# Attention by pairs of heads, and the out projection's first weights loaded during attention

## The chip, the cores and the metric

The kernel runs on one NeuronCore of a Trainium2 chip. The metric is the device time of one execution in microseconds (us); lower is better. The engines named below are TensorE (PE, matmuls; PEld is its weight load), VectorE (DVE), ScalarE (ACT), GpSimd (POOL) and SyncE (SP, which issues the DMAs). All run in parallel, each works through its own list in order, and they wait for each other on semaphores.

## The reference

Two layers of a decoder step in float32, for a prompt of 1024 tokens and 8 sample sequences of 4 new tokens each, all with the same weights. What matters here is the attention half of the mixer. Each token has 4 heads with a query of 128 values without rotation (nope) and 64 rotated values (rope); the keys come from a shared latent of 256 values and one rotated key of 64 that all heads share.

```python
s = einsum('bqhd,bkd->bhqk', q, lat) * scale          # causal, scale = (128 + 64) ** -0.5
p = softmax(s, axis=-1)
o = einsum('bhqk,bkr->bqhr', p, vals)                 # then W_uv, giving 128 values per head
x = x + concat([hm, ha], axis=-1) @ lw['w_out']       # hm: 4 mLSTM heads, ha: 4 attention heads
```

The sample tokens attend to 1024 past rows each, read from a paged cache through a page table (8 pages of 128 rows per sequence), and to the new rows of their sequence.

## The kernel before

The kernel keeps all activations with features on the 128 partitions and tokens along the columns (1024 prompt columns and 32 sample columns, NT = 1056). `build_program` (L2264) runs a loop over the two layers; each layer is a list of phases (`mix_projection`, `mla_prepare`, `mla_attend`, `out_projection`, `conv_ffn`, `layer_embedding`), and between phases all engines meet at a barrier (L142, L150), so that nothing of a phase starts before the one ahead is done. The residual x lies in DRAM during the mixer.

`mla_attend` (L1404) does the attention of the prompt in 32 blocks: 4 heads, and for each 8 query tiles i of 128 queries, which see (i + 1) * 128 keys. The list `blocks` (L1436) has all tiles of a head, then the next head. The order of the work is written out by hand per engine. For block n:

- PE, `scores(n)` (L1472): for each piece of up to 512 keys a nope matmul (L1480, contraction over 128 rows) and a rope matmul (L1481, over 64 rows, on partitions 0 to 63 for even heads and 64 to 127 for odd ones) into a PSUM bank. Blocks alternate between two sets of two banks. `scores(n + 1)` is issued ahead of the rest of block n.
- DVE, `maxima(n)` (L1684): the causal mask on the diagonal tile (L1689), the row maximum (L1694) and its scaling (L1696).
- ACT (L1671): the exponential with the row sum. DVE (L1734, L1736): the reciprocal of the sum and the product with it.
- PE, `turned(n)` (L1495): each 128x128 tile of the probabilities is transposed (L1502), up to four into a bank; ACT, `transposed(n)` (L1621), copies each group of up to four out (L1627).
- PE, `values(n)` (L1485): one matmul per tile (L1491) into bank 6; DVE, `output(n)` (L1699), copies the result into `cat` (L1702).

An fp32 matmul is two records in the trace (two LDWEIGHTS and two MATMUL); a transpose is one.

Between these blocks `sample(n)` puts the sample tokens' attention into the same lists, in steps that all use PSUM bank 7. Two groups of four sequences take 11 steps each (GAP), the first at block FIRST = 8. Step 0 does the new scores, steps 1 and 2 the past scores (L1540, L1543, which need the cached pages), step 3 the softmax, steps 4 to 6 transposes (L1554), 7 and 8 the past values (L1567), 9 and 10 the heads' outputs (L1577, L1586). `absorbed` (L1506), at block 1, prepares the sample queries.

SP loads the pages with `load_pages` (L1394): for each sequence eight page numbers are read (L1397), then eight DMAs issued (L1402). The first four sequences come at the start; the keys of the other four after the first group's past scores (`past_done` 2), their latents after the first group's past values (`so_done` 1), into the same four page tiles.

`out_projection` (L1748) multiplies the 8 head outputs in `cat` with w_out. Products are made of two halves in a reduced format, three matmuls each (`product3`, L208): the high half of weights and activations is a copy by ACT, the low half a subtraction by DVE. `WeightRing` (L170) stages four weight jobs of 1 MB (JW = 2048 columns) in two slots. SP loads jobs 0 and 1, then x (4.2 MB), then the rest (L1763 to L1767); ACT splits job 0 (L198), then the 8 heads (L1773), DVE subtracts (L204, L1787), and PE's first job (L210) starts with the first head's low half. Job 1's subtraction on DVE stands behind the arrival of x (L1789).

## Time and profile before

| what | us |
|---|---|
| median of 3 runs | 3328.66 |
| lowest and highest of them | 3320.07, 3329.58 |
| the profiled execution | 3329.29 |
| its span in the trace | 3327.5 |
| PE busy (share of the span) | 3087.8 (93%) |
| DVE, ACT, POOL busy | 1524.3, 1067.3, 144.3 |
| mean granted TensorE clock, share of full | 0.958 |
| attention, layer 1 and layer 2 | 183.6, 186.6 |

The trace has one execution of the program. Times count from the start of the span. The first layer's attention lies at 416.9 to 600.5, the second's at 2052.3 to 2238.9. PEclk is the clock that TensorE was granted: 1.00 is 2.4 GHz, 0.50 is 1.2 GHz. Matmuls overlap in the engine, so the distance from one start to the next is the cost of one in a dense stretch, not its duration. An idle time is that of the engine just before the instruction, with what ended it behind the arrow.

### The profile page before, as it was taken

How to read it: one execution, taken by the hardware profiler on the slowest of the kernel's cores; microseconds unless marked ns; L12 is line 12 of the kernel's file. 1: busy time of each engine (PE TensorE's matmuls, PEld its weight loads, DVE VectorE, ACT ScalarE, POOL GpSimd, SP SyncE). 2: the span in 40 equal slices, each digit the busy share in tenths (PEclk: the TensorE clock that was granted, in tenths of full speed). 3: DMA queues.
4: the chain of work that ended last, by engine and by line, in shares of the span. 5: the costliest groups of instructions: out<-in, count | busy, mean ns of one | idle time of the engine just before them, and what ended most of it. 6: DMA issues, size and time to landing. Idle time of an engine off the chain costs nothing. (4 is left out here: it accounts for less than half of the span.)

```text
span 3327.5 us, 49163 instructions
## 1 busy us (share of the span) xinstructions
PE 3087.8 (93%) x19219; PEld 2874.2 (86%) x19219; DVE 1524.3 (46%) x2458; ACT 1067.3 (32%) x1982; POOL 144.3 (4%) x260
## 2 busy tenths in 40 slices
PE   4999999889999999988989999989899999999887
PEld 4998755789999999988989986559899999999886
DVE  4223643345454554447351345434554544454653
ACT  4323332324333323334242342322432323233341
POOL 0000300000000000000000012000000000000000
PEclk9999999889999999998989988989899999999988
DMA  5101252211111111102131023421111111111023
GB/s 212 52 26 44 86 172 70 103 56 51 39 39 52 46 44 51 39 18 90 40 123 41 16 99 101 133 60 81 68 40 50 51 39 51 39 39 51 6 103 131
DMA packets 60916, 220.53 MB, mean 66 GB/s; under 512 B 6922, under 2 KB 26890, under 8 KB 45842
## 3 DMA queue, kind: packets, MB, share of 16 engines
q1 hardware_dynamic: 60690, 217.27, 18.5%
q8 instruction: 172, 2.82, 0.4%
q14 instruction: 54, 0.44, 0.0%
HBM read 189.72 MB, written 27.52 MB: 65 GB/s over the span
## 5 line engine op out<-in xcount | busy, mean ns | idle before, releaser
L210 PE MATMUL psum<-h_high,conv_ffn_weight_parts 128*128 128x352 f32 x2112 | 690.4, 327 | 21.9 <-DVE h_low L315 14.3
L212 PE MATMUL psum<-h_high,conv_ffn_weight_parts 128*128 128x352 f32 x2112 | 686.7, 325 | 0.0
L211 PE MATMUL psum<-h_low,conv_ffn_weight_parts 128*128 128x352 f32 x2112 | 682.6, 323 | 0.0
L1990 DVE SCALAR_TENSOR_TENSOR conv_sum<-u_padded,vectors,conv_sum 128x1024 f32<-128x1024 f32 x176 | 226.1, 1285 | 595.1 <-ACT conv_sum L1939 582.6
L210 PEld LDWEIGHTS psum<-h_high,conv_ffn_weight_parts 128*128 128x128 f32 x2112 | 400.8, 190 | 24.9 <-issue 22.0
L211 PEld LDWEIGHTS psum<-h_low,conv_ffn_weight_parts 128*128 128x128 f32 x2112 | 399.3, 189 | 0.0
L212 PEld LDWEIGHTS psum<-h_high,conv_ffn_weight_parts 128*128 128x128 f32 x2112 | 397.1, 188 | 0.0
L210 PE MATMUL psum<-g_parts,conv_ffn_weight_parts 128*128 128x352 f32 x1056 | 345.3, 327 | 27.1 <-DVE g_parts L2001 16.3
L212 PE MATMUL psum<-g_parts,conv_ffn_weight_parts 128*128 128x352 f32 x1056 | 343.1, 325 | 0.0
L211 PE MATMUL psum<-g_parts,conv_ffn_weight_parts 128*128 128x352 f32 x1056 | 342.8, 325 | 0.0
L2009 DVE TENSOR_TENSOR x<-x,psum 128x352 f32<-128x352 f32 x528 | 255.5, 517 | 118.3 <-PE psum L212 117.9
L1935 ACT ACTIVATE u_padded<-psum 128x352 f32<-128x352 f32 (+1 forms) x264 | 120.2, 455 | 541.0 <-PE psum L212 541.0
L210 PEld LDWEIGHTS psum<-g_parts,conv_ffn_weight_parts 128*128 128x128 f32 x1056 | 199.9, 189 | 33.5 <-issue 16.8
L210 PE MATMUL psum<-h_high,_projection_weight_parts 128*128 128x352 f32 x576 | 192.5, 334 | 14.3 <-DVE h_low L315 14.3
L1948 ACT ACTIVATE g_parts<-conv_sum 128x1056 fp32r<-128x1056 f32 x44 | 47.8, 1087 | 486.9 <-PE psum L212 404.6
L211 PEld LDWEIGHTS psum<-g_parts,conv_ffn_weight_parts 128*128 128x128 f32 x1056 | 199.8, 189 | 0.0
L212 PEld LDWEIGHTS psum<-g_parts,conv_ffn_weight_parts 128*128 128x128 f32 x1056 | 198.9, 188 | 0.0
L212 PE MATMUL psum<-h_high,_projection_weight_parts 128*128 128x352 f32 x576 | 188.1, 326 | 0.0
L211 PE MATMUL psum<-h_low,_projection_weight_parts 128*128 128x352 f32 x576 | 187.7, 326 | 0.0
L1939 ACT ACTIVATE conv_sum<-psum,vectors 128x352 f32<-128x352 f32 x264 | 170.5, 646 | 0.1
L204 DVE TENSOR_TENSOR conv_ffn_weight_parts<-conv_ffn_weight_stage,conv_ffn_weight_parts 128x2048 fp32r<-128x2048 f32 x66 | 151.1, 2290 | 23.9 <-ACT conv_ffn_weight_parts L198 23.9
L210 PE MATMUL psum<-heads_high,_projection_weight_parts 128*128 128x352 f32 x384 | 126.0, 328 | 24.5 <-DVE heads_low L1787 24.5
(330 smaller groups left out, 5389.5 us busy)
## 6 DMA issues: line engine op xcount, KB each, us to landing
conv_ffn_weight_stage<-w_up_dram SPq DMA_DIRECT2D x44, 1024.0 KB, 4.8
conv_ffn_weight_stage<-w_down_dram SPq DMA_DIRECT2D x22, 1024.0 KB, 4.8
_projection_weight_stage<-w_in_dram SPq DMA_DIRECT2D x18, 1024.0 KB, 4.8
pages<-cache_dram SPq DMA_DIRECT2D x64, 288.0 KB, 4.2
pages<-cache_dram SPq DMA_DIRECT2D x64, 160.0 KB, 2.5
mix_work<-x_residual SPq DMA_DIRECT2D x16, 528.0 KB, 3.8
x<-x_residual SPq DMA_DIRECT2D x2, 4224.0 KB, 17.0
x_residual<-x SPq DMA_DIRECT2D x16, 528.0 KB, 2.7
```

The lines of the kernel that those rows point to most:

```text
L204: dve.tensor_tensor(dst[:, 1, 0:width], self.stage[:, slot % self.stages, 0:width], dst[:, 0, 0:width].bitcast(F32), ALU.subtract).then_in ...
L210: pe.matmul(out, lhs[0], rhs[0], start=first, stop=False)
L211: pe.matmul(out, lhs[0], rhs[1], start=False, stop=False)
L212: return pe.matmul(out, lhs[1], rhs[0], start=False, stop=last)
L1935: act.activation(u[:, q, 2 + c * CH:2 + c * CH + n], src[:, 0:n], ACT.Copy)
L1939: op = act.activation(t[:, q, chunk(c)], src, ACT.Identity, bias=bias, scale=w2)
L1948: act.activation(gp[:, 0, slot, :], t[:, 1, :], ACT.Copy).then_inc(ph["ghi_made"], 1)
L1990: dve.scalar_tensor_tensor(t[:, q, 0:SEQ], row[:, tap:tap + SEQ], w, t[:, q, 0:SEQ], ALU.mult, ALU.add).then_inc(ph["conv_step"], 1)
L2009: dve.tensor_tensor(X[:, k, chunk(c)], X[:, k, chunk(c)], ps[:, (6 + n) % 8, 0:CH], ALU.add).then_inc(ph["x_made"], 1)
```

## The change

Attention now works through pairs of blocks: the same query tile of two neighbouring heads (`blocks`, 16 pairs). PE issues the two nope matmuls of a piece of keys, then the two rope matmuls, which lie on partitions 0 to 63 and 64 to 127 and go to different banks. A pair's scores wait for both exponentials of the pair before (`exp_done` 2p). Behind them PE transposes the probabilities of the pair before, does a sample step, the values of both blocks (side by side in bank 6) and another sample step. ACT alternates the copies of the transposes with the exponentials; DVE does both maxima, both normalizations, and one copy out per pair. The sample steps start at block 9 (FIRST), `absorbed` is at block 3, and the row maximum of the sample comes one block earlier. Scratch tiles move: the sample's probabilities and latent output to `core.norm`, two transposed tiles to the place of the absorbed weights.

SP loads the first two weight jobs of w_out in the attention phase, once the second group's past values are read (`so_done` 2), into a stage of its own (`out_stage`, just below x), and waits for them before the phase ends. `out_projection` takes this stage over, issues x first, and splits jobs 0 and 1 without a wait.

```diff
--- before.py
+++ after.py
@@ -1401,14 +1401,14 @@
-def mla_attend(nc, core, ckv, kr, qn, qr, kn, vt, cat, pages):
+def mla_attend(nc, core, ckv, kr, qn, qr, kn, vt, cat, pages, out_stage):
...
     QT = SEQ // P
-    FIRST, GAP = QT, 11
+    FIRST, GAP = 9, 11
     B_TR, B_OUT, B_SAMPLE = 4, 6, 7
@@ -1417,10 +1417,10 @@
         uv = at(M_CKV + NT, "w_uv", [P, 2, A_HEADS * A_DV])
-        spr = at(M_QK, "probs_s", [P, ROW + NS])
-        o = at(M_QK, "o_latent", [P, KV_RANK])
-        spT = at(M_KN, "probs_s_T", [P, N_PAGES, P])
-        oT = at(M_KN, "o_latent_T", [P, 2, P])
+        spr = core.norm
+        o = core.norm[:, 0:KV_RANK]
+        spT = at(M_CKV, "probs_s_T", [P, N_PAGES, P])
+        oT = at(M_CKV, "o_latent_T", [P, 2, P])
         take = core.slab.bump(M_PAGES + 4 * PW)
@@ -1428,12 +1428,13 @@
             nc, s_done=1, masked=1, max_step=1, neg_made=1, exp_done=1, rec_step=1, p_made=1, tr_done=1, pt_made=1,
-            o_done=1, o_used=1, uk_loaded=1, uv_loaded=1, pages_loaded=4, keys_loaded=4, latents_loaded=4, zeroed=1, ql_done=1,
+            o_done=1, o_used=1, uk_loaded=1, uv_loaded=1, pages_loaded=4, keys_loaded=4, latents_loaded=4, out_loaded=1, zeroed=1, ql_done=1,
             q_made=1, new_done=1, new_made=1, past_done=1, past_made=1, row_step=1, sexp_done=1, str_done=1,
...
         bank = ps[:, B_SAMPLE, :]
-        blocks = [(h, i) for h in range(A_HEADS) for i in range(QT)]
+        blocks = [(2 * hp + b, i) for hp in range(A_HEADS // 2) for i in range(QT) for b in range(2)]
+        PAIRS = len(blocks) // 2
         groups = [[(n, j0, min(j0 + 4, i + 1)) for j0 in range(0, i + 1, 4)] for n, (h, i) in enumerate(blocks)]
@@ -1456,6 +1457,11 @@
                 load_pages(sp, core, 4 + q, pages[q], ph["latents_loaded"][q], keys=False)
+            sp.wait_ge(ph["so_done"], 2)
+            for j in range(2):
+                sp.dma_start(out_stage[:, j, :], core.w_out[ds1(l), j].rearrange("l p n -> (l p) n"))\
+                  .then_inc(ph["out_loaded"], 16)
+            sp.wait_ge(ph["out_loaded"], 32)
@@ -1469,28 +1475,33 @@
         def _(pe):
-            def scores(n):
-                h, i = blocks[n]
-                if n >= 2:
-                    pe.wait_ge(ph["exp_done"], n - 1)
-                keys = (i + 1) * P
+            def scores(p):
+                if p:
+                    pe.wait_ge(ph["exp_done"], 2 * p)
+                h0, i = blocks[2 * p]
+                queries, keys = slice(i * P, (i + 1) * P), (i + 1) * P
                 for c in range(0, keys, 512):
                     w = min(512, keys - c)
-                    out = ps[:, 2 * (n % 2) + c // 512, 0:w]
-                    pe.matmul(out, qn[:, h, i * P:(i + 1) * P], kn[:, h, c:c + w], start=True, stop=False)
-                    mm = pe.matmul(out, qr[part(h), h // 2, i * P:(i + 1) * P], kr[part(h), c:c + w],
-                                   start=False, stop=True)
-                mm.then_inc(ph["s_done"], 1)
+                    out = [ps[:, 2 * b + c // 512, 0:w] for b in range(2)]
+                    for b in range(2):
+                        pe.matmul(out[b], qn[:, h0 + b, queries], kn[:, h0 + b, c:c + w], start=True, stop=False)
+                    for b in range(2):
+                        mm = pe.matmul(out[b], qr[part(b), h0 // 2, queries], kr[part(b), c:c + w],
+                                       start=False, stop=True)
+                        if c + w == keys:
+                            mm.then_inc(ph["s_done"], 1)
...
                 h, i = blocks[n]
+                b = n % 2
                 pe.wait_ge(ph["pt_made"], first_group[n + 1])
-                if n:
-                    pe.wait_ge(ph["o_used"], n)
+                if b == 0:
+                    pe.wait_ge(ph["o_used"], n // 2)
                 for j in range(i + 1):
-                    mm = pe.matmul(ps[:, B_OUT, 0:P], vt[:, j, h * P:(h + 1) * P],
-                                   pT[:, n % 2, j * P:(j + 1) * P], start=(j == 0), stop=(j == i))
-                mm.then_inc(ph["o_done"], 1)
+                    mm = pe.matmul(ps[:, B_OUT, b * P:(b + 1) * P], vt[:, j, h * P:(h + 1) * P],
+                                   pT[:, b, j * P:(j + 1) * P], start=(j == 0), stop=(j == i))
+                if b:
+                    mm.then_inc(ph["o_done"], 1)
@@ -1589,7 +1600,7 @@
                 gr, s = divmod(n - FIRST, GAP)
-                if n == 1:
+                if n == 3:
                     absorbed()
@@ -1606,21 +1617,23 @@
-            scores(0)
-            for n in range(len(blocks)):
-                if n + 1 < len(blocks):
-                    scores(n + 1)
-                if n:
-                    values(n - 1)
-                sample(n)
-                turned(n)
-            values(len(blocks) - 1)
+            for p in range(PAIRS + 1):
+                if p < PAIRS:
+                    scores(p)
+                if p:
+                    turned(2 * p - 2)
+                    turned(2 * p - 1)
+                sample(2 * p)
+                if p:
+                    values(2 * p - 2)
+                    values(2 * p - 1)
+                sample(2 * p + 1)
...
                 if n >= 2:
-                    act.wait_ge(ph["o_done"], n - 1)
+                    act.wait_ge(ph["o_done"], n // 2)
                 for m, (_, j0, j1) in enumerate(groups[n]):
@@ -1638,7 +1651,7 @@
                 gr, s = divmod(n - FIRST, GAP)
-                if n == 1:
+                if n == 3:
                     absorbed()
@@ -1662,20 +1675,26 @@
-            for n, (h, i) in enumerate(blocks):
+            def probabilities(n):
+                h, i = blocks[n]
+                b = n % 2
                 act.wait_ge(ph["neg_made"], n + 1)
...
                     act.wait_ge(ph["p_made"], n - 1)
-                b = n % 2
                 act.activation(pr[:, b, 0:(i + 1) * P],
...
                    .then_inc(ph["exp_done"], 1)
-                if n:
-                    transposed(n - 1)
-                sample(n)
-            transposed(len(blocks) - 1)
+            for p in range(PAIRS + 1):
+                for n in (2 * p, 2 * p + 1):
+                    if p:
+                        transposed(n - 2)
+                    if p < PAIRS:
+                        probabilities(n)
+                sample(2 * p)
+                sample(2 * p + 1)
@@ -1696,11 +1715,20 @@
-            def output(n):
+            def normalized(n):
                 h, i = blocks[n]
-                dve.wait_ge(ph["o_done"], n + 1)
-                dve.tensor_copy(cat[:, 4 + h, i * P:(i + 1) * P], ps[:, B_OUT, 0:P])\
-                   .then_inc(ph["o_used"], 1)
+                b = n % 2
+                dve.wait_ge(ph["exp_done"], n + 1)
+                dve.reciprocal(mx[:, b, 3:4], mx[:, b, 2:3]).then_inc(ph["rec_step"], 1)
+                dve.wait_ge(ph["rec_step"], n + 1)
+                dve.tensor_scalar(pr[:, b, 0:(i + 1) * P], pr[:, b, 0:(i + 1) * P], mx[:, b, 3:4], None,
+                                  ALU.mult).then_inc(ph["p_made"], 1)
+            def output(p):
+                h, i = blocks[2 * p]
+                dve.wait_ge(ph["o_done"], p + 1)
+                dve.tensor_copy(cat[:, 4 + h:6 + h, i * P:(i + 1) * P],
+                                ps[:, B_OUT, 0:2 * P].rearrange("p (h n) -> p h n", h=2)).then_inc(ph["o_used"], 1)
@@ -1711,7 +1739,7 @@
                        .then_inc(ph["new_made"], 1)
-                elif s == 3:
+                elif s == 2:
                     dve.wait_ge(ph["past_made"], 2 * gr + 2)
@@ -1727,25 +1755,19 @@
-            maxima(0)
-            for n, (h, i) in enumerate(blocks):
-                b = n % 2
-                dve.wait_ge(ph["exp_done"], n + 1)
-                dve.reciprocal(mx[:, b, 3:4], mx[:, b, 2:3]).then_inc(ph["rec_step"], 1)
-                dve.wait_ge(ph["rec_step"], n + 1)
-                dve.tensor_scalar(pr[:, b, 0:(i + 1) * P], pr[:, b, 0:(i + 1) * P], mx[:, b, 3:4], None,
-                                  ALU.mult).then_inc(ph["p_made"], 1)
-                if n >= 2:
-                    output(n - 2)
-                if n + 1 < len(blocks):
-                    maxima(n + 1)
-                sample(n)
-            output(len(blocks) - 2)
-            output(len(blocks) - 1)
-def out_projection(nc, core, cat, X):
+            for p in range(PAIRS + 1):
+                if p < PAIRS:
+                    for n in (2 * p, 2 * p + 1):
+                        maxima(n)
+                    for n in (2 * p, 2 * p + 1):
+                        normalized(n)
+                sample(2 * p)
+                if p:
+                    output(p - 1)
+                sample(2 * p + 1)
+def out_projection(nc, core, cat, X, stage):
@@ -1755,29 +1777,27 @@
         squares = Squares(take, ph, core, "out_projection")
-        ring = WeightRing(take, ph, "out_projection")
+        ring = WeightRing(take, ph, "out_projection", stage=stage)
         ps = core.psum
...
         def _(sp):
-            ring.load(sp, 0, core.w_out[ds1(l), 0].rearrange("l p n -> (l p) n"), JW)
-            ring.load(sp, 1, core.w_out[ds1(l), 1].rearrange("l p n -> (l p) n"), JW)
             sp.dma_start(X[:], core.x_dram).then_inc(ph["x_loaded"], 16)
...
         def _(act):
-            ring.hi(act, 0, JW)
+            ring.hi(act, 0, JW, loaded=False)
             for k in range(KX):
                 act.activation(catp(0, k), cat[:, k, :], ACT.Copy).then_inc(ph["chi_made"], 1)
-            ring.hi(act, 1, JW)
+            ring.hi(act, 1, JW, loaded=False)
             for j in range(4):
...
                 if j + 2 < 4:
-                    ring.hi(act, j + 2, JW, (ph["mm_done"], 6 * (j + 1)))
+                    ring.hi(act, j + 2, JW, (ph["mm_done"], 6 * (j + 1)), half=0)
@@ -2248,6 +2268,7 @@
         self.rt = at(M_KROT + NT + 72, "mla_rt", [P, 2, 2, TT])
+        self.out_stage = at(X_AT - 2 * JW, "out_weight_stage", [P, 2, JW])
         self.qT = at(M_QK, "m_q", [P, 2, NT])
@@ -2291,9 +2312,10 @@
             pages = [core.slab.at(M_PAGES + i * PW, f"pages_{i}", [P, PW]) for i in range(4)]
-            mla_attend(nc, core, mem.ckv, mem.kr, mem.qn, mem.qr, mem.kn, mem.vt, mem.cat, pages)
+            mla_attend(nc, core, mem.ckv, mem.kr, mem.qn, mem.qr, mem.kn, mem.vt, mem.cat, pages,
+                       mem.out_stage)
             X = core.slab.at(X_AT, "x", [P, KX, NT])
-            out_projection(nc, core, mem.cat, X)
+            out_projection(nc, core, mem.cat, X, mem.out_stage)
             conv_ffn(nc, core, X)
...
```

## Rows read from the trace of the kernel before

**Rows 1.** The page's head and its part 1, PE alone

```profile
span 3327.5 us, 49163 instructions
...
PE 3087.8 (93%) x19219; PEld 2874.2 (86%) x19219; DVE 1524.3 (46%) x2458; ACT 1067.3 (32%) x1982; POOL 144.3 (4%) x260
```

**Rows 2.** Busy time per stretch: attention of both layers, and layer 1 from 462.5

```profile
core 0: us, PE busy (x) PEld busy (x) DVE busy (x) ACT busy (x) POOL busy (x), PEclk, DMA share, GB/s
416.90:600.50 183.60, 171.15 (x1018) 102.09 (x1018) 70.81 (x204) 54.92 (x132) 2.63 (x9) 0.93 0.36 110
2052.30:2238.90 186.60, 174.38 (x1018) 103.46 (x1018) 70.78 (x204) 54.94 (x132) 2.63 (x9) 0.91 0.35 108
462.50:600.50 138.00, 127.71 (x807) 75.89 (x805) 51.22 (x145) 40.46 (x95) 0.00 (x0) 0.94 0.24 70
```

**Rows 3.** PE's waits in layer 1's attention: total, times, longest

```profile
PE psum L1491 <- DVE heads_out L1702: 10.6, 6, 4.0
```

**Rows 4.** Timeline of PE in one block: start, us, what

```profile
434.31 0.94 PE L1491 MATMUL psum<-probs_T,a_v 128*128 128x128 f32 x6
435.08 0.60 PE L1502 MATMUL psum<-constants,probs 128*128 128x128 f32 x4
435.52 1.02 PE L1480 MATMUL psum<-a_k,a_q_nope 128*128 128x512 f32 x2
436.48 1.12 PE L1481 MATMUL psum<-k_rope,a_q_rope 64*128 64x512 f32 x2
...
438.16 0.70 PE L1481 MATMUL psum<-k_rope,a_q_rope 64*128 64x256 f32 x2
438.78 0.38 PE L1491 MATMUL psum<-probs_T,a_v 128*128 128x128 f32 x1
```

**Rows 5.** From attention to the out projection: timelines of DVE, SP, ACT, PE

```profile
600.19 0.29 DVE L1702 COPY heads_out<-psum 128x128 f32<-128x128 f32 x1 [5.88 <-PE psum L1491]
601.51 0.85 SPq L187 DMA_DIRECT2D _projection_weight_stage<-w_out_dram  x2
...
606.88 1.91 ACT L198 ACTIVATE _projection_weight_parts<-_projection_weight_stage 128x2048 fp32r<-128x2048 f32 x1 [10.56 <-DMA _projection_weight_stage<-w_out_dram]
...
612.43 0.63 PE L210 MATMUL psum<-heads_high,_projection_weight_parts 128*128 128x352 f32 x1 [12.28 <-DVE heads_low L1787]
```

**Rows 6.** Groups by line: the rope matmuls in layer 1's attention

```profile
L1481 PE MATMUL psum<-k_rope,a_q_rope 64*128 64x512 f32 (+3 forms) x96 | 44.4, 543 | 0.0
```

**Rows 7.** Timeline of PE in the phase before: one tile, and alternating halves

```profile
352.96 0.49 PE L1106 MATMUL psum<-m_v,ss_decayed 32*32 32x129 f32 x3
353.38 1.95 PE L1109 MATMUL psum<-state_sample,qs_by_sequence 64*32 64x129 f32 x32
```

**Rows 8.** Timelines of PE and SP, and one stretch: when the pages come

```profile
462.56 1.92 PE L1540 MATMUL psum<-pages,q_absorbed 128*32 128x512 f32 x16
...
422.39 33.14 SPq L1402 DMA_DIRECT2D pages<-cache_dram  x32
...
475.68 71.29 SPq L1402 DMA_DIRECT2D pages<-cache_dram  x64
...
460.00:461.00 1.00, 1.00 (x29) 0.65 (x27) 0.43 (x3) 0.18 (x1) 0.00 (x0) 1.00 0.31 123
```

**Rows 9.** Timelines of DVE and ACT at the widest block

```profile
587.59 0.30 DVE L1689 TENSOR_TENSOR psum<-psum,constants 128x128 f32<-128x128 f32 x1 [3.51 <-PE psum L1481]
587.92 1.22 DVE L1694 TENSOR_REDUCE softmax_rows<-psum 128x1 f32<-128x1024 f32 x1
...
589.37 1.11 ACT L1671 ACTIVATE probs<-psum,softmax_rows 128x1024 f32<-128x1024 f32 x1 [5.09 <-DVE softmax_rows L1696]
...
590.48 0.97 ACT L1627 ACTIVATE probs_T<-psum 128x512 f32<-128x512 f32 x2
```

**Rows 10.** A turn from one head to the next: PE's timeline, the stretch

```profile
547.66 3.33 PE L1491 MATMUL psum<-probs_T,a_v 128*128 128x128 f32 x14 [4.00 <-DVE heads_out L1702]
...
545.60:552.30 6.70, 4.63 (x22) 4.67 (x23) 1.83 (x7) 1.95 (x5) 0.00 (x0) 0.50 0.31 85
```

## The prediction

> **What bounds the kernel now.** I read the page first: a span of 3327.5 us with TensorE (PE) busy for 93% of it [rows 1]. The change touches the attention stage and the start of the out projection, each run once per layer, so I then took the busy time per stretch. Attention is 183.6 us in the first layer and 186.6 in the second, and PE is busy in it for 171 and 174 us [rows 2]. The list of PE's waits leaves it only 10.6 us of waiting on others per layer [rows 3]: the stage is PE's, except at its ends. Then the timeline of PE, for what a score matmul costs. A matmul is two records. At 512 columns a rope pair of records takes 1.05 us to the next start, at 256 columns 0.62 [rows 4]. So 256 columns cost 0.43 us, 1.68 ns per column, and 0.20 us per matmul is left that no column explains. It shows at each step from the 128-row form to the 64-row form and back, while transposes follow each other at 0.11 us and the six value records cost 0.77 (six times 0.11 and one such step). Outside attention, PE stands idle for 12.3 us before the out projection, behind the weights' DMA [rows 5].
>
> **The change, part by part.** *Score matmuls.* A layer has 48 rope matmuls (96 records [rows 6]), four heads of 12 column pieces, over 4 x 36 tiles of 128 columns. By pairs, the two no-rope matmuls stand side by side, then the two rope matmuls, on rows 0 to 63 and 64 to 127 and in different banks. Steps between forms fall from 96 to 48: 48 x 0.20 = 9.6 us. The rope columns cost 18432 x 1.68 ns = 31.0 us; if both run at once, 15.5 goes. The trace has such a pair at 32 output columns: 32 records of 129 columns on alternating row halves start within some 1.7 us, 0.054 each, where three on one tile take 0.11 each [rows 7]. That is two at once, and I take it for 128 output columns as well; the other bound is no overlap, a gain of 0, also kept. Together 25.1 us of PE work per layer. The Trainium skill's page TensorE: Matmul & The Clock Gate (Part 3) gives four packed row tiles as 3.07 times as fast, not 4; at three quarters of the ideal the 15.5 would be an estimated 12.
>
> *What comes back: the cached pages.* PE first needs them at 462.56 [rows 8]. SP issues their 32 DMAs until 455.5, and the DMA share falls inside 460 to 461 [rows 8]; so they landed at about 460.3 and PE had 2.3 us to spare. FIRST moves this step to block 10, behind the scores of pair 5. Up to there both orders do 42 score tiles, but the new one saves 4.5 us of overlap (21 x 0.215) and 14 steps (2.8), and has 17 value tiles (3.8) and 7 transposes (0.8) still before it: it arrives 11.9 us earlier, at 450.7 plus waits of its own, and stands until 460.3. So I count from there. The old order needs 138.0 us from 462.5 to the end [rows 2]. The new one saves 102/144 of 15.5 = 11.0 and 34 steps = 6.8, and adds the deferred 4.6: 124.8, end at 585.1.
>
> *Waits inside.* Scores of a pair now wait for both exponentials of the last pair; the banks of one block no longer fill while the other's are read. At the widest block [rows 9]: mask and maximum 1.8 us, twice; the first exponential ends at 3.3, the second at 5.7, behind two copies. PE meanwhile has 16 transposes (1.8) and 16 value tiles (3.5), and waits for the copies of the second head, which stand behind the first exponential on ScalarE (ACT), until 4.8: it is done at 6.4, a wait of 1.1 us. I take 0.6 us on average over the 11 pairs left, 7 us. Against that, two of three turns from a head's last block to the next head's first go. One costs 4.0 us of waiting and 6.7 us at half clock with 4.6 us of work in them, so 2.3 more [rows 10]. With a smaller one and the tail, I take 9 gone, 7 added, net -2: end at 583.1, 17.4 us less than 600.5. Bounds of this net: -8 and +6.
>
> *SP's queue.* The 64 further page loads issue over 71 us [rows 8], after a start of some 5 us; the sample work must end on them. In the new order the last latents land near 548, and PE wants them, counted back from 583 over the last two and a half pairs, near 550. They fit by little; late by 3 us, it costs 3. VectorE (DVE) copies two heads in one instruction, at no cost: PE does not wait for it with a pair between. FIRST, the sample's row maximum one block earlier and the moved scratch tiles add no instruction.
>
> *Early weights.* Both DMAs are now issued once the last past values are read, some 20 us before the end, and nothing else is on the queues. ACT splits the first weight at 606.88 where the DMA issue stood at 601.51 [rows 5]: 5.4 us go. What follows is a chain (split 1.9, subtraction 2.3, one head's split) that stays. x no longer shares the queues with 2 MB and is wanted only after eight subtractions of 1.2 us. PE starts at half clock either way: 0 (bounds -1 and +1).
>
> **Sum.** 17.4 + 5.4 = 22.8 per layer, 45.6 in two. The profiled execution took 3329.3 us (span 3327.5), 0.6 above the median: 3329.3 - 45.6 = 3283.7, so 3284.
>
> **The rivals.**
> *The rope pair does not overlap.* For it: no 64-row form with 128 output columns ever follows its like in the trace. Against: [rows 7]. 11.0 us come back per layer, some 3 of which cover waits: 9.4 + 5.4 = 14.8, twice, gives 3300.
>
> *Slower: PE stands behind the softmax of every pair.* If the second exponential has to end before the values of the pair before, PE has only the transposes to cover it: at the widest pair 5.7 - 1.8 = 3.9 us, at the narrowest some 2 (two short chains of mask, maximum and exponential). Mean 2.9, times 16, 47 us per layer against 30.5 gained: 3362. It decides from a mean wait of 1.9 us per pair. Against it: ACT copies the second head's transposes ahead of the second exponential, and the widest block gives 1.1 [rows 9].
>
> *The clock falls more often.* A pair puts up to 16 transposes and a short wait in a row, and the granted clock drops to 1.2 GHz after such a stretch: it did at 545.6 [rows 10], after a wait of 4 us. Once more at each of the 8 widest pairs, for 3.4 us, costs 1.7 x 8 = 13.6 per layer: 3311. Against: transposes at 435 run at 0.11 us each amid full clock [rows 4], and the new waits are short. The Trainium skill (TensorE: Matmul & The Clock Gate, Part 4) says transposes do not count as PE being busy; by that rule this case is the likely one, and the trace shows full clock beside runs of four only.
>
> *The early load does nothing:* ACT or DVE, not the DMA, would then hold the first matmul. The trace names the DMA as ACT's releaser after 10.6 us [rows 5], so this is unlikely: 3294.5.
>
> **How the numbers follow.** Forecast 0.73 (3270 to 3294); no overlap 0.13; clock 0.06; early load void 0.04; slower 0.04. The predicted time is the forecast's. The low end, 3270, takes the net of the waits at -8, which gives 3272, and the clock's -1. The high end, 3303, takes in no overlap with late latents; clock and softmax, one in ten, stay out. About 0.3% (10 us) is what a measurement of this kernel tells from no change. Faster 0.94; the same 0.02, from the edges of the clock case; slower 0.04.
>
> **What would show it.** Rope records of two heads starting within 0.02 us; some 3 us of PE per 512 columns of a pair's scores (1.72 + 0.86 + two steps of 0.20); a wait of PE for pages of 3 to 7 us near block 10; attention of about 166 us in layer one and 169 in layer two; PE waiting under 7 us per layer for the pair's exponentials and copies; idle before the out projection of 6.9 us instead of 12.3; the weights landed before attention ends. Wrong would be: rope records one after another (3300), waits above 1.9 us per pair, or a granted clock in attention below 0.85.

## The result, and the profile after

| | before | after |
|---|---|---|
| median | 3325.6 us (4 runs, 3320.1 to 3329.6) | 3281.2 us (4 runs, 3280.9 to 3281.9) |
| ratio, 95% interval | | 0.9869 [0.9854, 0.9884] |
| span of the profiled execution | 3327.5 us | 3280.1 us |

The change takes 44 us, 1.3%. The forecast was 3284.0 with a range of 3270 to 3303. To answer why, the two spans are compared, which differ by 47.4 us.

The page of the changed kernel, its head and the first line of part 1, against [rows 1]:

```profile
span 3280.1 us, 49103 instructions
...
PE 3042.8 (93%) x19219; PEld 2854.0 (87%) x19219; DVE 1520.0 (46%) x2426; ACT 1069.5 (33%) x1982; POOL 143.5 (4%) x260
```

PE's busy time is down by 45.0 us at the same 19219 instructions: the gain is less time for the same matmuls, not a shorter list. Some of it is clock: the trace has 260.8 us at half clock in the whole span where it had 282.1, 13.6 of the difference in attention. DVE has 32 instructions fewer (two heads' outputs in one copy). The busy time by stretch says where, against [rows 2] (length, then PE, PEld, DVE, ACT, POOL busy, the granted clock, DMA share, GB/s). The first two rows are attention of the two layers, the last two divide layer 1 where PE starts on the cached pages:

```profile
core 0: us, PE busy (x) PEld busy (x) DVE busy (x) ACT busy (x) POOL busy (x), PEclk, DMA share, GB/s
415.10:582.50 167.40, 150.48 (x1018) 93.10 (x1018) 68.33 (x188) 55.73 (x132) 2.59 (x9) 0.93 0.43 133
2032.20:2199.50 167.30, 151.61 (x1018) 94.52 (x1018) 68.30 (x188) 55.65 (x132) 2.52 (x9) 0.93 0.42 133
...
458.99:582.46 123.47, 115.33 (x842) 71.70 (x842) 47.64 (x123) 40.83 (x92) 0.00 (x0) 0.96 0.32 95
415.13:458.99 43.86, 35.15 (x177) 21.38 (x178) 20.69 (x65) 14.87 (x40) 2.56 (x9) 0.83 0.74 240
```

Attention takes 16.2 us less in layer 1 and 19.1 less in layer 2 (by first and last instruction: 183.5 to 167.3, 186.5 to 167.4). PE is busy for 20.7 and 22.8 us less in it, so some 4 us of what PE saved per layer came back as idle time (12.3 and 12.1 us of it before, 16.8 and 15.7 now). The rest of the 47.4 is ahead of the out projection, 5.5 us per layer (below): 16.2 + 19.1 + 10.9 = 46.2.

The timeline of PE at the widest pair (start, duration, what, count), which answers to [rows 4]:

```profile
562.87 1.88 PE L1487 MATMUL psum<-a_k,a_q_nope 128*128 128x512 f32 x4
564.68 1.13 PE L1489 MATMUL psum<-k_rope,a_q_rope 64*128 64x512 f32 x4
565.74 1.98 PE L1487 MATMUL psum<-a_k,a_q_nope 128*128 128x512 f32 x4
567.66 1.13 PE L1489 MATMUL psum<-k_rope,a_q_rope 64*128 64x512 f32 x4
568.72 0.98 PE L1513 MATMUL psum<-constants,probs 128*128 128x128 f32 x7
570.21 0.96 PE L1513 MATMUL psum<-constants,probs 128*128 128x128 f32 x7 [0.51 <-ACT probs_T L1640]
```

From the start of the rope records to the next start is 1.06 us (564.68 to 565.74), for four records; before, two took 1.05 [rows 4]. The second head's rope adds 0.01 us. The group of rope matmuls in layer 1's attention, a row of the groups by line, shows the same against its 44.4 us in [rows 6]:

```profile
L1489 PE MATMUL psum<-k_rope,a_q_rope 64*128 64x512 f32 (+3 forms) x96 | 23.3, 565 | 0.0
```

PE's waits in layer 1's attention, against [rows 3] (total, times, longest):

```profile
PE psum L1513 <- ACT probs_T L1640: 4.5, 8, 0.7
PE psum L1501 <- ACT probs_T L1640: 3.6, 10, 0.6
PE psum L1551 <- DMA pages<-cache_dram: 3.2, 1, 3.2
PE psum L1487 <- ACT probs L1685: 2.1, 1, 2.1
PE psum L1578 <- DMA pages<-cache_dram: 0.8, 1, 0.8
```

The 10.6 us behind `heads_out` are gone. In their place stand 8.1 us in 18 short waits for ACT's copies of the transposes, one wait of 2.1 for exponentials (at the very first pair, with nothing to cover it), 4.0 for the DMA of the pages, and 1.8 in three waits of the sample's steps that the rows leave out. The pages' wait is the one that is new in kind. The timelines of SP and of PE, which answer to [rows 8]:

```profile
420.53 33.15 SPq L1402 DMA_DIRECT2D pages<-cache_dram  x32
...
474.38 70.66 SPq L1402 DMA_DIRECT2D pages<-cache_dram  x64
560.14 0.89 SPq L1462 DMA_DIRECT2D out_weight_stage<-w_out_dram  x2
```

```profile
458.99 3.64 PE L1551 MATMUL psum<-pages,q_absorbed 128*32 128x512 f32 x16 [3.21 <-DMA pages<-cache_dram]
```

SP issues the page loads as slowly as before (33.15 us for 32, against 33.14), and PE, which is now quicker, stands for the last of them. Sixteen records then take 3.64 us where the same took 1.92 in [rows 8]: the granted clock is 0.50 from 457.9 to 464.7, so the wait of 3.2 us has a tail of half clock. Of the stretches the first two are layer 1's at half clock after its start, the third is its last pairs, and the fourth is one more at half clock that only layer 2 has, among its last pairs:

```profile
457.90:464.70 6.80, 5.71 (x34) 2.04 (x35) 0.62 (x1) 0.31 (x1) 0.00 (x0) 0.50 0.13 51
512.50:515.90 3.40, 3.40 (x22) 1.39 (x24) 1.04 (x4) 0.38 (x1) 0.00 (x0) 0.50 0.70 183
516.00:582.40 66.40, 61.64 (x465) 38.90 (x452) 27.82 (x70) 24.06 (x53) 0.00 (x0) 1.00 0.28 86
2188.40:2191.90 3.50, 3.50 (x19) 3.50 (x19) 1.18 (x4) 0.82 (x2) 0.00 (x0) 0.51 0.00 0
```

At the end of attention the timelines of DVE, ACT, DVE and PE, against [rows 5]:

```profile
582.03 0.42 DVE L1730 COPY heads_out<-psum 128x256 f32<-128x256 f32 x1 [5.49 <-PE psum L1501]
...
583.38 1.91 ACT L198 ACTIVATE _projection_weight_parts<-out_weight_stage 128x2048 fp32r<-128x2048 f32 x1 [4.21 <-PEq L142]
...
587.53 2.42 DVE L1807 TENSOR_TENSOR heads_low<-heads_out,heads_high 128x1056 fp32r<-128x1056 f32 x2
...
588.93 0.63 PE L210 MATMUL psum<-heads_high,_projection_weight_parts 128*128 128x352 f32 x1 [6.94 <-DVE heads_low L1807]
```

The weights were issued at 560.14, so ACT's split follows the barrier at once and not a DMA. From the end of the last copy (582.46) to PE's first matmul are 6.5 us; before, 12.0 (600.48 to 612.43). The chain of split, subtraction and first head that is left fills them. The out projection itself is no shorter for it: 97.3 us from its first matmul to the next phase before, 97.6 and 96.4 in the two layers now.

### The profile page after: what moved, and what is told of

Same layout as the page of the kernel before. It is cut to its first block and busy times, and to the rows that moved or that the text cites. A ratio compares the mean times of both kernels' runs of the same rounds, so it can differ in the third digit from the quotient of the medians.

```text
span 3280.1 us, 49103 instructions
## 1 busy us (share of the span) xinstructions
PE 3042.8 (93%) x19219; PEld 2854.0 (87%) x19219; DVE 1520.0 (46%) x2426; ACT 1069.5 (33%) x1982; POOL 143.5 (4%) x260
## 3 DMA queue, kind: packets, MB, share of 16 engines
q1 hardware_dynamic: 60690, 217.27, 18.7%
## 5 line engine op out<-in xcount | busy, mean ns | idle before, releaser
L210 PE MATMUL psum<-h_high,conv_ffn_weight_parts 128*128 128x352 f32 x2112 | 690.6, 327 | 21.2 <-DVE h_low L315 14.4
L210 PEld LDWEIGHTS psum<-g_parts,conv_ffn_weight_parts 128*128 128x128 f32 x1056 | 200.1, 189 | 33.6 <-issue 16.9
L1968 ACT ACTIVATE g_parts<-conv_sum 128x1056 fp32r<-128x1056 f32 x44 | 47.8, 1087 | 487.0 <-PE psum L212 404.6
L210 PE MATMUL psum<-h_high,_projection_weight_parts 128*128 128x352 f32 x576 | 192.3, 334 | 14.4 <-DVE h_low L315 14.4
L204 DVE TENSOR_TENSOR conv_ffn_weight_parts<-conv_ffn_weight_stage,conv_ffn_weight_parts 128x2048 fp32r<-128x2048 f32 x66 | 151.2, 2290 | 23.9 <-ACT conv_ffn_weight_parts L198 23.9
```

Source lines behind the costliest of these rows:

```text
L204: dve.tensor_tensor(dst[:, 1, 0:width], self.stage[:, slot % self.stages, 0:width], dst[:, 0, 0:width].bitcast(F32), ALU.subtract).then_in ...
L210: pe.matmul(out, lhs[0], rhs[0], start=first, stop=False)
L1968: act.activation(gp[:, 0, slot, :], t[:, 1, :], ACT.Copy).then_inc(ph["ghi_made"], 1)
```

## The experiments

Beside each kernel's median (of at least 4 runs) stands its ratio to the kernel before, from runs on the same chip (3325.5 us for the first four, 3325.6 for the others). Attention is given for both layers. As a stretch of half clock doubles what runs in it and its length differs from one kernel to the next, "at full clock" is the length of attention less half of the time that the trace shows at 0.50 in it. This is a rough correction, as it takes that time to be all work. Where PE's work alone is compared, it is PE's busy time less half of what of it lies at 0.50.

| kernel | median, us | ratio, 95% interval | attention, layers 1 and 2 | of it at 0.50 | at full clock |
|---|---|---|---|---|---|
| before | 3325.6 | 1 | 183.5, 186.5 | 27.3, 34.1 | 169.8, 169.5 |
| after | 3281.2 | 0.9869 [0.9854, 0.9884] | 167.3, 167.4 | 23.9, 23.9 | 155.4, 155.4 |
| load_only | 3309.3 | 0.9948 [0.9928, 0.9969] | 186.6, 181.1 | 34.1, 20.5 | 169.5, 170.8 |
| pairs_only | 3293.8 | 0.9903 [0.9883, 0.9922] | 166.8, 168.0 | 23.9, 20.5 | 154.9, 157.8 |
| rope_serial | 3324.6 | 0.9996 [0.9985, 1.0007] | 193.6, 184.9 | 47.8, 27.3 | 169.6, 171.3 |
| heads_apart | 3292.6 | 0.9908 [0.9882, 0.9933] | 173.3, 173.7 | 17.1, 20.5 | 164.8, 163.4 |
| first_7 | 3296.4 | 0.9919 [0.9896, 0.9943] | 173.8, 173.1 | 27.3, 23.9 | 160.1, 161.1 |
| first_11 | 3271.6 | 0.9839 [0.9820, 0.9858] | 162.1, 164.0 | 13.7, 20.5 | 155.3, 153.7 |
| turned_first | 3279.1 | 0.9862 [0.9838, 0.9886] | 166.6, 165.3 | 23.9, 17.1 | 154.7, 156.7 |
| turned_first11 | 3270.2 | 0.9840 [0.9817, 0.9864] | 160.7, 160.2 | 17.1, 10.2 | 152.2, 155.1 |

**load_only: the early load alone, in the kernel before.**

```diff
             for q in range(4):
                 load_pages(sp, core, 4 + q, pages[q], ph["latents_loaded"][q], keys=False)
+            sp.wait_ge(ph["so_done"], 2)
+            for j in range(2):
+                sp.dma_start(out_stage[:, j, :], core.w_out[ds1(l), j].rearrange("l p n -> (l p) n"))\
+                  .then_inc(ph["out_loaded"], 16)
+            sp.wait_ge(ph["out_loaded"], 32)
...
-        ring = WeightRing(take, ph, "out_projection")
+        ring = WeightRing(take, ph, "out_projection", stage=stage)
...
```

> The kernel before, with the early load of the projection's first two weight jobs alone. Theory: the 5.4 us of DMA wait at the out projection's start go in each layer, nothing else moves: 3325.6 - 11 = 3314 to 3315 us. Rival (the first matmul is held by the clock or by x's load as well): less than 4 us in all, 3322 or more.

Measured: 3309.3 us, 16 less than before. The time from attention's last copy to the first matmul is 6.47 us in both layers, as in the changed kernel. So the load takes 2 x 5.5 = 11 us in its own place, and works without the pairs. That is more than the 3314 to 3315 expected, and the other 5 us are not of its making in any way that a row shows. Attention took 3.1 us more in layer 1 and 5.4 less in layer 2, with 6.8 us more and 13.6 less at half clock, and no less work at full clock (159.0 and 159.4 us, 159.2 and 159.0 before). The trace has 24.4 us less of half clock in the whole span, 17.6 of them outside attention.

**pairs_only: the pairs alone.**

```diff
-            sp.wait_ge(ph["so_done"], 2)
-            for j in range(2):
-                sp.dma_start(out_stage[:, j, :], core.w_out[ds1(l), j].rearrange("l p n -> (l p) n"))\
...
+            ring.load(sp, 0, core.w_out[ds1(l), 0].rearrange("l p n -> (l p) n"), JW)
+            ring.load(sp, 1, core.w_out[ds1(l), 1].rearrange("l p n -> (l p) n"), JW)
             sp.dma_start(X[:], core.x_dram).then_inc(ph["x_loaded"], 16)
...
```

> The changed kernel with the weights loaded in the out projection again. Theory: the two parts add, 3281.2 + 11 = 3292 us, and attention stays at 167 us per layer. Rival (the parts share a gain, for one because both end the same idle stretch or the same clock fall): nearer to 3281 or over 3297.

Measured: 3293.8 us, 32 less than before and 12.6 more than the changed kernel. The idle time ahead of the out projection is back at 11.92 us in both layers, and attention is 166.8 and 168.0 us, as with the load. This is the 3292 expected of two parts that add. The 16 and 32 us make 48, where together they gave 44, but 5 of the 16 are not the load's (above).

**rope_serial: pairs, but each head's rope behind its nope.** The order of the work, the waits and the early load stay; the rope records have no neighbour on the other half of the rows, and a layer has its 96 steps between forms again.

```diff
                     for b in range(2):
                         pe.matmul(out[b], qn[:, h0 + b, queries], kn[:, h0 + b, c:c + w], start=True, stop=False)
-                    for b in range(2):
                         mm = pe.matmul(out[b], qr[part(b), h0 // 2, queries], kr[part(b), c:c + w],
```

> The changed kernel with the matmuls of a piece in the order nope, rope, nope, rope: no overlap and 96 steps between forms again, the pair schedule as it is. Theory: up to 25.1 us of TensorE work per layer come back, 5 to 8 of them into waits: 17 to 20 us per layer, 3315 to 3321 us; against heads_apart the 48 steps are 8 to 10 us per layer. Rival (the pair schedule itself, with fewer turns from head to head, makes most of the gain): below 3300.

Measured: 3324.6 us in 10 runs, 43 more than the changed kernel and above the 3315 to 3321 expected. The whole gain of the pairs hangs on the order of four instructions, and the order by pairs has no worth without it: against load_only, which does the same work head by head, the kernel is even 15 us slower. At full clock the two are alike (169.6 and 171.3 us against 169.5 and 170.8); of the 15 us, 10.3 are half of the 20.5 us more that it spends at 0.50. The order by pairs does take waits away: PE is idle for 8.3 and 8.7 us here, where it was for 12.3 and 12.1 in the kernel before. But with the same 96 steps its work is 162.0 and 162.8 us, 3 to 4 more than before, which gives that back. The timeline of PE at the widest pair:

```profile
588.93 1.02 PE L1487 MATMUL psum<-a_k,a_q_nope 128*128 128x512 f32 x2
589.88 1.12 PE L1488 MATMUL psum<-k_rope,a_q_rope 64*128 64x512 f32 x2
590.93 1.12 PE L1487 MATMUL psum<-a_k,a_q_nope 128*128 128x512 f32 x2
...
596.21 1.12 PE L1488 MATMUL psum<-k_rope,a_q_rope 64*128 64x512 f32 x2
597.26 0.98 PE L1512 MATMUL psum<-constants,probs 128*128 128x128 f32 x7
```

The scores of the pair take 8.33 us (588.93 to 597.26) where the changed kernel takes 5.85 (562.87 to 568.72).

**heads_apart: pairs of heads h and h + 2.** Both rope keys then lie on the same 64 partitions, while the rope matmuls still stand next to each other in the list: no overlap, 48 steps between forms.

```diff
-        blocks = [(2 * hp + b, i) for hp in range(A_HEADS // 2) for i in range(QT) for b in range(2)]
+        blocks = [(hp + 2 * b, i) for hp in range(A_HEADS // 2) for i in range(QT) for b in range(2)]
...
-                        mm = pe.matmul(out[b], qr[part(b), h0 // 2, queries], kr[part(b), c:c + w],
+                        mm = pe.matmul(out[b], qr[part(h0), b, queries], kr[part(h0), c:c + w],
...
```

> The changed kernel with heads h and h + 2 as a pair: both rope matmuls then lie on the same 64 partitions and cannot run at once, while order, waits, and steps between matmul forms stay. Theory: 15.5 us of TensorE work come back per layer, of which waits on the copies of the transposes and on the pages cover up to half: 7.5 to 15.5 us per layer, 3296 to 3312 us. Rival (the gain is the order and the fewer steps, the overlap is worth nothing): within 3 us of 3281.

Measured: 3292.6 us (3288.7 to 3302.2), 11.4 more than the changed kernel, which is under the 3296 to 3312 expected, and 32 less than rope_serial. Its timeline at the widest pair:

```profile
564.75 1.88 PE L1487 MATMUL psum<-a_k,a_q_nope 128*128 128x512 f32 x4
566.57 1.98 PE L1489 MATMUL psum<-k_rope,a_q_rope 64*128 64x512 f32 x4
568.48 1.98 PE L1487 MATMUL psum<-a_k,a_q_nope 128*128 128x512 f32 x4
570.39 1.98 PE L1489 MATMUL psum<-k_rope,a_q_rope 64*128 64x512 f32 x4
572.30 0.87 PE L1513 MATMUL psum<-constants,probs 128*128 128x128 f32 x6
```

From 564.75 to 572.30 are 7.55 us. These three timelines price both terms at one place, all at full clock. Rope_serial to heads_apart: 0.78 us for four steps fewer, 0.195 each. Heads_apart to the changed kernel: 1.70 us for 1024 columns that run beside others, 1.66 ns per column. The records of a group say where: four rope records take 1.91 us to the next start here (570.39 to 572.30), 1.06 in the changed kernel.

In the whole kernel the two terms weigh otherwise than in PE's work. Busy time and granted clock of attention, layers 1 and 2, of rope_serial and of heads_apart:

```profile
417.45:611.00 193.55, 185.26 (x1018) 103.89 (x1018) 71.00 (x188) 53.55 (x132) 2.56 (x9) 0.88 0.36 115
2055.02:2239.95 184.93, 176.21 (x1018) 99.91 (x1018) 70.88 (x188) 53.56 (x132) 2.56 (x9) 0.93 0.38 120
```

```profile
414.35:587.68 173.33, 162.74 (x1018) 101.32 (x1018) 69.12 (x188) 53.70 (x132) 2.55 (x9) 0.95 0.41 128
2032.46:2206.11 173.65, 163.78 (x1018) 101.37 (x1018) 69.30 (x188) 53.69 (x132) 2.55 (x9) 0.94 0.41 128
```

Idle time is length less busy time: 10.6 and 9.9 us in heads_apart, 16.9 and 15.7 in the changed kernel. PE's work is 154.9 and 154.3 us in heads_apart, 140.0 and 140.2 in the changed kernel. So the overlap took 14.9 and 14.1 us of work out, some 6 us of idle time per layer came in, and 17 us are left in the two layers; by the table's last column it is 9.4 and 8.0. Attention is only 12.3 us shorter because the changed kernel has 10.2 us more at half clock in it (worth 5.1).

The 32 us between rope_serial and heads_apart are more than the 2 x 48 x 0.195 = 18.7 us of its steps, for the clock: 75.1 us at 0.50 in the two layers against 37.6. Half of the difference is 18.8 us. What is left of the difference in attention is 4.8 and 7.9 us per layer. In PE's work it is 7.1 and 8.5, where 48 x 0.195 is 9.4, and 2.3 and 1.2 us of idle time came in.

**first_7 and first_11: the sample work one pair earlier or later.**

```diff
-    FIRST, GAP = 9, 11
+    FIRST, GAP = 11, 11
```

> The changed kernel with the sample steps one pair later (FIRST 11). Theory: TensorE reaches the cached pages after they have landed, so the 3.2 and 2.0 us of waiting go, and with them the clock fall that follows the wait (3.4 to 6.8 us at half clock, worth 2 to 3 us) : 8 to 12 us in all, 3269 to 3273. The steps that move to the end fill waits there. Rival (the wait only changes its place: the tail gets the sample's last steps, the latents come as late as before): 3278 to 3284.

> The changed kernel with the sample steps one pair earlier (FIRST 7). Theory: TensorE waits for the pages some 8 us longer per layer, since the pair that goes behind the wait is no longer before it, and the stage is longer by that: 16 to 20 us in all, 3297 to 3301. Rival (the pages are no bound, TensorE's work is, and the wait of 3 us is only its slack): under 6 us, 3287 or less.

Measured: 3271.6 us with 11 (3269 to 3273 expected), 3281.2 with 9, 3296.4 with 7 (3297 to 3301 expected). The step on the pages, as PE's timeline has it, with 7:

```profile
457.08 3.64 PE L1551 MATMUL psum<-pages,q_absorbed 128*32 128x512 f32 x16 [11.30 <-DMA pages<-cache_dram]
```

and with 11:

```profile
466.84 1.92 PE L1551 MATMUL psum<-pages,q_absorbed 128*32 128x512 f32 x16
```

Against the start of attention PE begins that step after 42.4 us with 7, after 43.9 with 9, and after 48.7 with 11. The first two numbers are SP's, which needs 5.4 us to start and 32 to 33 to issue 32 loads; with 11, PE itself is the later. A pair later the wait of 3.2 us is gone and the half clock behind it too (the records take 1.92 us, not 3.64); a pair earlier it is 11.3 us. With 11 the latents of the second group are late instead, by 2.5 us in place of 0.8, as SP's second batch starts 61.8 us into attention and not 59.3, while the rest of PE's list has become shorter:

```profile
PE psum L1513 <- ACT probs_T L1640: 4.5, 8, 0.7
PE psum L1501 <- ACT probs_T L1640: 4.1, 10, 0.6
PE psum L1578 <- DMA pages<-cache_dram: 2.5, 1, 2.5
PE psum L1487 <- ACT probs L1685: 2.1, 1, 2.1
```

With 7, the wait of 11.3 us (11.6 in layer 2) makes attention 6.5 and 5.7 us longer, and first_7 is 15 us slower in all: the pages do bound the stage there. The 10 us of first_11 have another makeup. Attention is 5.2 and 3.4 us shorter, but at full clock, by the table, only 0.1 and 1.7, as the wait for the latents came in. Nearly all of the gain is half clock: 240.4 us of it in the whole span against 260.8. Part of that lies ahead of the first sample step, where both kernels have the same list: layer 1 begins with 13.7 us at half clock in the changed kernel and with 6.8 in first_11. Why is not shown.

**turned_first: the first head's transposes ahead of the next pair's scores**, so that ACT can copy them in the meantime.

```diff
             for p in range(PAIRS + 1):
+                if p:
+                    turned(2 * p - 2)
                 if p < PAIRS:
                     scores(p)
                 if p:
-                    turned(2 * p - 2)
                     turned(2 * p - 1)
```

> The changed kernel with the transposes of a pair's first head issued ahead of the next pair's scores, so that ScalarE copies them under those scores. Theory: the waits of TensorE on these copies (4.5 and 3.6 to 4.1 us per layer) go, but the transposes now wait for the normalized probabilities, which come about as late, so little is left: between 3276 and 3284. Rival: the copies were the only thing, the whole 16 us go, 3265 to 3269.

Measured: 3279.1 us, 2 less than the changed kernel, within the spread of the runs (3274.8 to 3284.0). PE's waits in layer 1:

```profile
PE psum L1501 <- ACT probs_T L1641: 11.3, 10, 1.5
PE psum L1551 <- DMA pages<-cache_dram: 3.0, 1, 3.0
PE psum L1513 <- DVE probs L1725: 2.1, 1, 2.1
```

The waits between groups of transposes (L1513 for ACT, 4.5 us) are down to 0.4, as meant. But the values now wait for 11.3 us in place of 3.6. The wait has moved: fewer instructions of PE are left between the scores and the values, and ACT still copies the second head's transposes behind the next pair's first exponential.

**turned_first11: both.**

```diff
-    FIRST, GAP = 9, 11
+    FIRST, GAP = 11, 11
...
+                if p:
+                    turned(2 * p - 2)
                 if p < PAIRS:
                     scores(p)
                 if p:
-                    turned(2 * p - 2)
                     turned(2 * p - 1)
```

> Both of the last but one and the first edit of this call: transposes of the first head ahead of the next scores, and the sample steps one pair later. Theory: the gains add if they are different waits, so first_11's time less what turned_first gains; 3265 to 3275. Rival (what one edit takes out of the stage's first third the other one puts into the wait for the pages): no better than the better of the two.

Measured: 3270.2 us (3266.7 to 3274.9). It is the fastest kernel here by its median, 11 us under the changed one, but not to be told from first_11 (3270.0 to 3272.7), which needs one number changed. So the runs do not decide between gains that add, 3269.5 us, and the rival, the better of the two.

## Why the forecast held, point by point

**Steps between forms, 9.6 us per layer: right in price.** The 0.20 us, read from gaps that no column explained, is 0.195 where four steps are taken away and nothing overlaps on either side. The Trainium skill (TensorEngine Tiling (Array Packing), Key Properties) says that changing the tiling mode drains the engine; the runs agree in that each change costs time, 0.195 us a step here.

**Overlap of the rope columns, 15.5 us per layer: right.** It was inferred from records with 32 output columns [rows 7], and holds with 128: 1.70 us at the widest pair where 1.72 was worked out, 14.9 and 14.1 us of work in the two layers. The estimate of 12 by the page on packed tiles (the Trainium skill, TensorE: Matmul & The Clock Gate, Part 3) was too low for two tiles of 64 rows; the measurement decides.

**PE's work, 25.1 us per layer in all: too high.** From the kernel before to the changed one it fell by 19.2 and 18.8 us (159.2 and 159.0 to 140.0 and 140.2). The overlap is in it with its 14 to 15, so the steps and the new order brought 4 to 5 and not 9.6. What the sum left out is that the order by pairs has a price of its own, the 3 to 4 us that rope_serial shows. Part of it is likely the end of a group ahead of a wait: seven transposes take 0.98 us there (568.72) where 0.11 each make 0.77, and layer 1 has 8 such waits before and 24 now. The rest is open.

**The pages: right in place and time.** PE was to arrive at 450.7 plus waits, and to stand until 460.3. It arrived at 455.8 (its waits up to there are 2.1 + 2.6 + 0.7 = 5.4 us) and stood until 459.0, 43.9 us into attention where 43.3 was forecast. From there to the end it took 123.5 us; the forecast had 124.8 less 2. The waits of 3.2 us in layer 1 and 2.0 in layer 2 lie at and under the low end of "3 to 7". That a wait there is a real cost and not slack is shown by first_7; first_11, which takes it away, is 10 us faster, mostly by half clock.

**Waits inside: near in size, off in place.** "I take 0.6 us on average over the 11 pairs left, 7 us" named the values behind the copies of the second head. From the pages on these take 1.0 us. Another 3.8 stand between the first head's transposes and the second's (4.5 with the one ahead of the pages; 8 times, at most 0.7 us, in the pairs of five tiles and more): each group of up to four tiles takes a bank, there are two for them, and the pair's third group must wait for the copy of the first. This wait was not in the prediction at all. With 1.8 in the sample's steps and 0.8 for the latents it makes 7.4 us. Over the whole of attention PE waits 10.2 us for copies and exponentials, over the "under 7" of the signs, but 5.4 of it stand ahead of the pages and cost nothing, as PE would wait there for them. The 10.6 us behind `heads_out` did go.

**The latents: right.** They were to land near 548, when PE would want them near 550: "they fit by little". PE wanted them at 547.2 and they were there at 548.0, 0.8 us late.

**The early load, 5.4 us per layer: right.** The idle time fell by 5.5 us in each layer, in both kernels that have the load. The unforeseen gain in load_only is half clock, most of it outside attention.

**The net per layer, 17.4 us: right as a mean (16.2 and 19.1), partly by luck.** Two misses cancel. From the pages to the end of layer 1 the forecast took 13.2 us of work off (11.0 and 6.8 less the deferred 4.6) and 2 of waits and half clock; measured are 9.9 of work, 2.2 of waits and 2.5 of half clock, 14.5 us in place of 15.2. Half clock was counted at 2.3 us for one turn and less for another, alike in both layers, and nothing for the new stretch behind the pages (457.9 to 464.7). By the table attention at full clock is 14.4 and 14.1 us shorter; the rest is half clock, 27.3 to 23.9 us in layer 1 (worth 1.7) and 34.1 to 23.9 in layer 2 (worth 5.1). The layers differ in gain because the kernel before had 6.8 us more of it in layer 2.

**The rivals.** *No overlap* is out by the timelines, and its price, 3300, was too high: heads_apart, which is that case, takes 3292.6, 11.4 us above the changed kernel and not 16. Its 8 us per layer of work less waits are near what the table shows at full clock, 9.4 and 8.0: in layer 1 PE has no wait for pages without the overlap, and for copies ahead of the values only 1.3 us; with it, 4.0 and 3.6. What the price left out is half clock, of which heads_apart has 10.2 us less. *Behind every softmax* is out: exponentials hold PE once, for 2.1 us. *The clock falls more often*, at each of the 8 widest pairs of a layer, is out as a count, not as a case. In layer 1 the granted clock is 1.00 from 516.0 to 582.4, over up to 16 transposes in a row. In layer 2, with the same list, it falls once among the last pairs, at 2188.4 for 3.4 us, behind 14 transposes with a wait of 0.51 between them and a group with 16 columns; the same records at 568.7 to 572.7 in layer 1 left it at 1.00. The rule that transposes don't count as PE being busy (the Trainium skill, TensorE: Matmul & The Clock Gate, Part 4) is neither borne out nor refuted by this, and it cost at most 1.7 us. Apart from the stretch that begins 1.8 us into attention (416.9 to 430.6), the two falls in layer 1 come with waits: in the one for the pages (457.9), and behind two short ones of 0.6 and 0.5 us (512.5). *The early load does nothing* is out by load_only. A fifth reading, that the order by pairs is itself the gain because it has fewer turns, falls with rope_serial, which has that order and gains nothing in all.

## What to carry to other kernels

Matmuls on half of the rows belong next to each other in the list, on opposite halves (here in different banks; one bank was not tried): that, fewer steps and overlap together, was worth the whole change in attention, and the same loop with the four instructions in another order was worth nothing. Once PE is quicker, each load that was timed against its old pace has to be placed anew: the sample work moved by a pair gave another 10 us, though mostly by half clock, and a pair the other way cost 15. A sum of PE's work taken from one kernel's rows misses what a new order adds by itself, here 3 to 4 us of 160 per layer. And a wait taken off one instruction is worth only what the next one in the list does not wait for, as with the transposes moved ahead.

## What the runs showed of the hardware

**Two fp32 matmuls on 64 rows each, on opposite halves and next to each other in the list, run at once in full:** four records of 512 columns in 1.06 us, against 1.91 us when both heads lie on the same half.

**A step between the 128-row and the 64-row form costs 0.195 us,** as much as some 117 columns of an fp32 matmul (1.66 ns each).

**Half clock can last through dense work.** In layer 1 of rope_serial the granted clock stays at 0.50 from 419.5 to 453.7, 34.1 us, although PE is hardly ever idle in it (busy for 32.9 us of it). In the changed kernel it is over after 13.7 us, with more idle time (busy for 11.9). The rows of rope_serial (the same columns as above):

```profile
427.00:440.00 13.00, 12.89 (x40) 8.12 (x40) 3.78 (x13) 2.50 (x10) 0.00 (x0) 0.50 0.82 280
440.00:450.00 10.00, 10.00 (x18) 3.58 (x18) 2.97 (x8) 1.02 (x3) 0.00 (x0) 0.50 0.77 255
```

and of the changed kernel:

```profile
427.00:440.00 13.00, 11.37 (x46) 6.03 (x47) 5.84 (x19) 4.61 (x14) 0.00 (x0) 0.86 0.72 240
440.00:450.00 10.00, 9.35 (x73) 6.04 (x73) 5.46 (x16) 3.21 (x8) 0.00 (x0) 1.00 0.82 262
```

The first has more steps between forms and no rope records at once; what the clock goes by there stays open, and layer 2 of the same kernel left half clock after 20.5 us. Taken as half of the difference at 0.50, the clock makes 13.7 of the 43 us between rope_serial and the changed kernel, and 18.8 of the 32 to heads_apart: the price of an order, taken from whole times, can be nearly twice its price in PE's work.
